# The norms' conditioning products and sums of squares in another order, and the output read bank by bank

## The reference

```python
y = jnp.einsum('bse,ed->bsd', jnp.concatenate([ya, yb, yc], axis=-1), w_out[layer])
h = _layernorm(DEEPNORM_ALPHA * h + y, ln_g[layer], ln_b[layer])
```

```python
mod = silu(c) @ w_ada + b_ada            # 1024 x 6144
sh_m, sc_m, g_m, sh_f, sc_f, g_f = jnp.split(mod[:, None, :], 6, axis=-1)
h = _rms(x, norm_mix) * (1.0 + sc_m) + sh_m
```

## Time and profile before

| | |
|---|---|
| median of 3 runs | 1643.54 us (1640.99 to 1645.29) |
| the profiled execution | 1639.43 us, its span 1637.6 us |
| PE busy | 1545.6 us (94%) |
| DVE, ACT, POOL busy | 450.9, 278.3, 21.5 us |
| HBM read | 511.21 MB, 314 GB/s over the span |
| mean granted clock of TensorE | 0.995 |

### The profile page before, as it was taken

The page is one execution under the profiler, slowest core; times in us unless marked ns, Lnnn a source line. Parts: engine busy times, 40 slices in busy tenths (PEclk is TensorE's granted clock), DMA queues, the critical chain, the costliest instruction groups (busy, mean ns, idle before and its releaser), DMA issues.

```text
span 1637.6 us, 18468 instructions
## 1 busy us (share of the span) xinstructions
PE 1545.6 (94%) x7521; PEld 876.1 (53%) x7521; DVE 450.9 (28%) x970; ACT 278.3 (17%) x552; POOL 21.5 (1%) x42
## 2 busy tenths in 40 slices
PE   7999899998999999999999999999999998998997
PEld 6768688786887778853333333333333333333232
DVE  2453463512445381231211211121112112111111
ACT  1234114223222431030000000000000000000000
POOL 4000000000000000000000000000000000000000
PEclk9999999999999999999999999999999999999999
DMA  9762895247322424679999999999999999999996
GB/s 262 187 204 103 289 328 178 85 148 246 136 103 78 154 103 154 257 308 422 428 427 427 428 427 427 429 428 428 427 427 429 428 427 427 427 427 428 427 425 289
DMA packets 83785, 515.19 MB, mean 315 GB/s; under 512 B 5412, under 2 KB 8772, under 8 KB 59152
## 3 DMA queue, kind: packets, MB, share of 16 engines
q1 hardware_dynamic: 81456, 511.35, 76.7%
q0 software_dynamic: 2240, 3.02, 1.9%
q10 hardware_dynamic: 32, 0.01, 0.0%
HBM read 511.21 MB, written 3.15 MB: 314 GB/s over the span
## 4 chain that ended last, share of the span: by engine, by line
PE 78%; DMA 14%; DVE 5%; ACT 2%; issue 2%; SPq 0%; ACTq 0%; DVEq 0%
PE psum L486 27%; PE psum L1156 20%; PE psum L1253 11%; DMA ring<-in_w_gu 9%; DMA w_down<-in_w_gu 4%; PE psum L1137 4%; PE psum L495 3%; PE psum L1146 2%; PE psum L1104 2%; PE psum L526 1%; PE psum L552 1%; PE psum L1241 1%; DVE hidden L2223 1%; DMA ring<-in_w_ada 1%; ACT ls L1420 1%
## 5 line engine op out<-in xcount | busy, mean ns | idle before, releaser
L486 PE MATMUL psum<-spare,ring 128*128 128x256 f32 x1504 | 332.8, 381 | 4.6 <-ACT spare L1463 4.4
L486 PEld LDWEIGHTS psum<-spare,ring 128*128 128x128 f32 x1504 | 283.2, 190 | 52.6 <-issue 11.6
L1156 PE MATMUL psum<-ring,hg 128*64 128x512 f32 x1040 | 233.3, 596 | 7.4 <-DMA ring<-in_w_gu 7.3
L1156 PEld LDWEIGHTS psum<-ring,hg 128*64 128x64 f32 x1040 | 71.0, 137 | 156.3 <-issue 140.0
L1156 PE MATMUL psum<-w_down,hg 128*64 128x512 f32 x656 | 146.3, 596 | 4.8 <-DMA w_down<-in_w_gu 4.8
L2214 DVE TENSOR_SCALAR gu<-psum 128x512 f32<-128x512 f32 x32 | 22.1, 692 | 326.2 <-PE psum L1156 326.2
L2226 DVE TENSOR_TENSOR o_slot<-psum,gain_rows 128x512 f32<-128x512 f32 x32 | 22.1, 692 | 319.1 <-PE psum L1253 319.1
L1156 PEld LDWEIGHTS psum<-w_down,hg 128*64 128x64 f32 x656 | 44.8, 137 | 97.8 <-issue 88.6
L1253 PE MATMUL psum<-w_down,hiddenT 128*64 128x512 f32 x352 | 78.0, 595 | 9.5 <-ACT hiddenT L1696 7.2
L1253 PE MATMUL psum<-ring,hiddenT 128*64 128x512 f32 x352 | 78.0, 594 | 8.3 <-issue 8.3
L1690 ACT ACTIVATE putT<-psum 128x256 f32<-128x256 f32 x32 | 12.3, 384 | 380.9 <-PE psum L1163 380.8
(11 more groups left out here) (417 smaller groups left out, 1461.3 us busy)
## 6 DMA issues: line engine op xcount, KB each, us to landing
ring<-in_w_gu SPq DMA_DIRECT2D x65, 2048.0 KB, 28.0
w_down<-in_w_gu SPq DMA_DIRECT2D x41, 2048.0 KB, 28.2
ring<-in_w_in SPq DMA_DIRECT2D x24, 2048.0 KB, 9.1
w_down<-in_w_dn SPq DMA_DIRECT2D x22, 2048.0 KB, 28.6
ring<-in_w_dn SPq DMA_DIRECT2D x22, 2048.0 KB, 31.5
ring<-in_w_ada SPq DMA_DIRECT2D x12, 2048.0 KB, 9.2
spare<-in_w_gu SPq DMA_DIRECT2D x11, 2048.0 KB, 28.1
nine<-in_w_gu SPq DMA_DIRECT2D x11, 2048.0 KB, 29.6
```

What stands on the lines that cost most here:

```text
L486: mm = pe.matmul(bank[0:m, c * T:(c + 1) * T], w[:, k, c0 + c * P:c0 + c * P + m], src[:, k, :], start=(i == 0), stop=(i == k_n - 1))
L1156: mm = pe.matmul(psum[half * CAP:(half + 1) * CAP, loop_bank(4 + part), :], hg[:, k, side, :], w[:, c0:c0 + 512], start=False, stop=(k == ...
```

## The change

- In both layers' norms one group of `w_ada` is multiplied ahead of the sums of squares instead of two, and the three matmuls of `ada_parts` come behind the sums instead of ahead of them.
- Layer 0's norm takes two groups in all instead of three. The third, ada2, is multiplied in layer 1 behind the products of q1. Layer 1's norm takes one group ahead of the sums and two behind.
- Six of the eight sums of squares of the second block's first norm come ahead of the wait for `mod_rows` and of the turn into columns, two behind.
- The last `add_up` announces each bank, ScalarE copies each bank when it is announced, and the store is four DMAs of 256 KB, each behind its own copy, instead of two of 512 KB.

```diff
@@ norm_sums
             if aside:
                 ada(aside)
-                ada_parts()
             square_sums_of(tag, range(KC))
@@ layer: products of q and k
                 last_of(f"{name}{l}", f"{L}{name}1")
+                if (l, g) == (1, 0):
+                    ada(1)
@@ layer: end
-            norm_sums(L, [f"{L}out{j}" for j in range(4)], aside=2)
-            ada(1)
+            norm_sums(L, [f"{L}out{j}" for j in range(4)], aside=1)
+            ada_parts()
+            ada(1 if l == 0 else 2)
+        square_sums_of("m.", range(0, 6))
         pe.wait_ge(ev("mod_rows"), 1)
         bank = take("mod")
...
         full(mm, "mod")
-        norm_sums("m.", None)
+        square_sums_of("m.", range(6, KC))
@@ add_up
-        def add_up(side):
+        def add_up(side, last=False):
...
                                    start=False, stop=False, skip_group_check=True)
-            mm.then_inc(ev("added"), 1)
+                    if last:
+                        mm.then_inc(ev("rows_added"), 1)
+            if not last:
+                mm.then_inc(ev("added"), 1)
...
-        add_up(1)
+        add_up(1, last=True)
@@ SyncE, end
         for b in range(NB):
-            sp.wait_ge(ev("out_rows"), 2 * b + 2)
-            sp.dma_start(out[0, b * P:(b + 1) * P, :], h_tok[:, b, :]).then_inc(ev("out_done"), 16)
-        sp.wait_ge(ev("out_done"), 16 * NB)
+            for j in range(2):
+                sp.wait_ge(ev("out_rows"), 2 * b + j + 1)
+                sp.dma_start(out[0, b * P:(b + 1) * P, 512 * j:512 * j + 512], h_tok[:, b, 512 * j:512 * j + 512])\
+                    .then_inc(ev("out_done"), 16)
+        sp.wait_ge(ev("out_done"), 32 * NB)
@@ ScalarE, end
-                act.wait_ge(ev("added"), first + TOGETHER + NE)
+                act.wait_ge(ev("added"), first + TOGETHER + NE - 1)
...
-        act.wait_ge(ev("added"), NE)
         for b in range(NB):
             for j in range(2):
+                act.wait_ge(ev("rows_added"), 2 * b + j + 1)
                 act.activation(h_tok[:, b, 512 * j:512 * j + 512], psum[:, loop_bank(2 * b + j), :], ACT.Copy)\
```

## The result

| | before | with the change |
|---|---|---|
| median of 20 runs | 1643.4 us (1639.9 to 1649.17) | 1651.53 us (1646.09 to 1652.97) |
| profiled execution, its span | 1639.43, 1637.6 us | 1652.67, 1650.8 us |
| mean granted clock of TensorE | 0.995 | 0.989 |

The change is slower: 1.0049 times the time before, 95% interval 1.0041 to 1.0057, or 8.1 us by the medians. The forecast was +2.15 us, that is 1645.6, with a range from 1640 to 1649.5.

What follows compares the result with a forecast made beforehand. TensorE holds 78% of the chain of waits, DMA 14%; the experts are DMA-bound. Layer 0 to the scores +6.0, layer 1's norm -2.35 and the end -1.5 sum to +2.15 us: 1645.6 us, range 1640 to 1649.5.

Steps and rivals of the forecast that it cites:

- q1 holds the gap: Layer 0's norm: q1's load lands at 203.2 us, so its products start only then despite earlier sums; -0.4 us.
- Low clock behind the wait for q1: Layer 0: after 8.2 us idle, q1's products start at 1.2 GHz instead of 2.4; +1.9 us.
- No more waiting chunk by chunk for ScalarE: q1's 32 matmuls run at full pace, 13.8 us instead of 14.4; -0.55 us.
- ada2's own time and D4's late slot: Layer 1's start: ada2 adds 1.9 us behind q1; D4, issued later, delays the rope, 3.15 us of new wait.
- the wait for the rope: Before layer 1's first scores: TensorE waits for VectorE's rope, delayed by D5's late landing; 3.15 us.
- Layer 1's norm: Fewer matmuls ahead of the sums of squares let the second block's products start sooner; -2.35 us.
- 1.3 us of it is low clock escaped: Layer 1's norm: 1.3 us of its gain is that the sums ran at 1.2 GHz before.
- From there both engines and ScalarE shift alike, so nothing takes it back: After layer 1's first scores: the +6.0 us delay passes on unchanged.
- slower rival: New waits, for the rope and for rstd, each bring low clock costing 1.7 us; both give 1649.1 us; chance 0.14.
- The end: Last add_up: copies follow each bank and the last, smaller store is issued 1.3 us sooner; -1.5 us.

Runs made afterwards that it cites:

- e9: The change with q1's load issued ahead of ada2's; median 1639.6 us, the kernel before 1643.3.
- e3: The change with 18 matmuls nobody reads ahead of TensorE's wait for q1; median 1648.3 us, the kernel before 1644.0.
- e8: e1 with D4's load held until q1's products are done; median 1647.3 us, the kernel before 1643.9.
- e10: The kernel before with unread matmuls in three waits: layer 1's logf, second block's first products, its seventh head's scores; median 1639.5 us, the kernel before 1643.3.
- e11: The change with unread matmuls in five waits: e10's three, ahead of q1, ahead of layer 1's first scores; median 1639.2 us, the kernel before 1643.3.
- e1: The change with ada2 multiplied in layer 0's gap again, nothing behind q1; median 1641.6 us, the kernel before 1644.0.
- e5: e4 with 6 matmuls nobody reads in TensorE's wait ahead of the second block's first products; median 1639.5 us, the kernel before 1643.9.
- e6: e2 with two stores of 512 KB instead of four, banks still copied one by one; median 1644.2 us, the kernel before 1643.9.
- e4: The change with layer 0's norm as in the kernel before; median 1641.0 us, the kernel before 1644.0.
- e7: e1 with eight more 32x512 matmuls nobody reads behind q1's products; median 1649.8 us, the kernel before 1643.9.
- e2: The kernel before with the change's end alone (banks announced one by one, four stores); median 1641.4 us, the kernel before 1644.0.

## Why the prediction was wrong

- **q1 holds the gap** (-0.4): right, -0.3; e9 shows that the load was the cause.
- **Low clock behind the wait for q1** (+1.9): right, 1.75. e3 takes it away.
- **No more waiting chunk by chunk for ScalarE** (-0.55): too large. Without low clock and without ada2's own 1.9 us, e3's stretch from q1's products to the rotation is 27.9 us against 28.0 before, so 0.1 to 0.2 was won.
- **ada2's own time and D4's late slot** (with the three above +6.0 at the scores): right, 5.8 in the profile; the wait for the rope was 2.6 us instead of 3.15, and by luck that miss offsets the term above. e8 shows the slot's part alone, 2.9 us.
- **Layer 1's norm** (-2.35): right in the stage, -2.4. But the sentence that 1.3 us of it is low clock escaped overlooked where this low clock would go.
- **"From there both engines and ScalarE shift alike, so nothing takes it back"**: this step failed. The shift is passed on, but the prediction put what low clock costs at the later waits at nothing new, and it is no constant: from the scores to the first expert the change has 6.4 us more of TensorE's busy time, with the same matmuls, and the two stages take 6.5 us longer, leaving the norm's -2.4 aside. e10 and e11 show the cause: with fillers in the waits the 8.1 us between the two orders shrink to -0.3. The text had the mechanism as its slower rival, at two places and 1.7 us each, with a chance of 0.14. It is what happened, at two more places and with stretches up to 6.8 us, twice as long as the longest of the rows read: the price of each wait was taken from one execution. A stretch of 6.8 us at half the clock costs up to 3.4 us, and that should have been the upper end.
- **The end** (-1.5): its size failed. 0.4 us was won. The first copy starts 1.16 us after the matmuls' start and not 0.5 to 0.7, so the copies end 0.9 us sooner and not 1.3; and they met stores that went out or landed later.

The Trainium skill's rule (TensorE: Matmul & The Clock Gate, Part 1: The HAM clock gate), by which the throttled state is the default and activity releases it, was weighed only for q1's start. There the trace agrees with it: behind 8.42 us of waiting the clock was low until 210.4. The shorter waits were not weighed again, and the rows are divided on them: the one of 3.17 us had no low clock at its end in the three profiles of the old order without a filler, had it in all seven of the new order, and had none where a filler stood in it.

What stays open is why the stretches were 6.8 us long more often with the change. Its profile has four of that length, e1's three, e9's two, those of e3, e5, e6 and e8 one each, and that of the kernel before none, so it is no property of one place. The medians point the same way: 17 of the change's 20 runs lie above 1648.7, while e4, with the same last norms, has none above 1644.5.

## What to carry to other kernels

Before a chain is shortened, look up when the weights behind it land, and whose slot they and their followers wait for: moving the products without their loads won 0.3 us and cost a wait elsewhere, moving both won 5 in that stage (e9). Where TensorE has to wait two or three microseconds, give it products that nobody reads, into a bank that is free: three such fillers were worth 4 us in the kernel before, five were worth 12 in the changed one. A profile of one execution tells where low clock can fall, not what it costs on average.

## What was not expected of the hardware

- Eight matmuls of 32x512 that write to one group of 32 PSUM partitions take 6.6 us (e7, at full clock), and the same eight of the kernel, spread over four such groups, 1.9: in the trace of the kernel before the records of the four groups start within 0.02 us of each other, in e7 each starts 0.43 us behind the last.
- At the same wait the clock fell in some profiles and not in others, though the code around it is the same. Behind the 2.3 us for `logf` in layer 1 it stayed full in e7, was low for 3.4 us in the kernel before and for 6.8 us in the change; behind the wait for the rope it was low for 3.4 us in the change (2.56 us of waiting) and stayed full in e8 (2.75 us).
- The issue of one of four stores took 1.27 us (e2) and up to 1.77 us (e9) where the others took 0.35 to 0.46, and stores of 512 KB landed in 2.7 to 3.0 or in 3.5 to 3.7 us, depending on when they were issued.
